# A one-core transformer step on Trainium2: modulation blocks at other units, inverse sums four at a time, w_o loaded from inside the attention loop

## What is computed

```python
shift1, scale1, gate1, shift2, scale2, gate2 = jnp.split(mod, 6, axis=-1)   # mod = silu(c) @ w_ada + b_ada
h = rmsnorm(x, norm1) * (1 + scale1) + shift1
q_a, kv_a, k_r, u = jnp.split(h @ w_in, ...)
q = rmsnorm(q_a, q_norm) @ w_qb                    # 8 heads, 64 plain + 32 rotary columns
k_nope, v = split(rmsnorm(kv_a, kv_norm) @ w_kvb)  # rotary on q_rope, k_rope for latent tokens
attn = softmax(q @ k.T * ATTN_SCALE) @ v           # latent: over latent and cached context keys
pooled = pool_mix(u, w_pool, pool_scale)
x = x + gate1 * (concat(attn, pooled) @ w_o)
h2 = rmsnorm(x, norm2) * (1 + scale2) + shift2
x = x + gate2 * (square(relu(h2 @ w1)) @ w2)       # w1 is 1024 x 4096
```

## Time and profile before

| | us |
|---|---|
| Device time, median of 3 runs | 1407.33 |
| Lowest and highest | 1406.74, 1409.57 |
| The profiled execution | 1411.18 |
| Its span in the profile | 1409.4 |
| Opening | 0 to 187 |
| Attention loop | 187 to 484 |
| Output projection | 484 to 590 |
| MLP | 590 to 1409 |

### The profile page before, as it was taken

How to read it: one execution, slowest core, us unless ns; L and a number is a source line. 1 busy time by engine, 2 the same in 40 slices (tenths; PEclk the granted TensorE clock), 3 DMA queues, 4 the chain that set the end, 5 groups by cost and what they waited for, 6 DMA issues and landing times.

```text
span 1409.4 us, 20531 instructions
## 1 busy us (share of the span) xinstructions
PE 1366.4 (97%) x7548; PEld 1229.6 (87%) x7548; DVE 789.5 (56%) x1074; ACT 715.8 (51%) x1537; POOL 444.4 (32%) x533
## 2 busy tenths in 40 slices
PE   7999989999999899999999999999999999999996
PEld 1899879999998778899998889999999999999995
DVE  4777567777787634355554456544444565444444
ACT  4867578888888623233333443433334443333332
POOL 3366648888888444430000003100000030000002
PEclk9999899999999999999999999999999999999998
DMA  9431101111111430344443333533333334333321
GB/s 343 148 100 53 35 5 44 43 40 44 43 39 39 139 138 1 127 175 172 168 154 122 115 119 122 190 119 119 133 135 120 120 120 165 138 129 119 119 89 45
DMA packets 50493, 154.50 MB, mean 110 GB/s; under 512 B 9848, under 2 KB 12440, under 8 KB 50424
## 3 DMA queue, kind: packets, MB, share of 16 engines
q1 hardware_dynamic: 49560, 150.47, 30.6%
q0 software_dynamic: 864, 3.15, 0.5%
HBM read 148.60 MB, written 4.83 MB: 109 GB/s over the span
## 4 chain that ended last, share of the span: by engine, by line
PE 64%; POOL 1%; DMA 1%; DVE 0%; issue 0%; ACT 0%; DVEq 0%; POOLq 0%
PE bank L2075 29%; PE bank L2083 28%; PE bank L1796 6%; DMA x<-in_w_o 1%; PE bank L1558 1%; POOL x L1866 0%; PE bank L2097 0%; DVE wol L1753 0%; POOL stat L1870 0%; POOL stat L1890 0%; ACT woh L1722 0%; DVE x L2026 0%; DVE xn L2014 0%; POOL stat L1872 0%; DVEq L1807 0%
## 5 line engine op out<-in xcount | busy, mean ns | idle before, releaser
L2075 PE MATMUL bank<-h2h,w1l 128*128 128x384 f32 x768 | 258.3, 336 | 0.0
L2075 PE MATMUL bank<-h2l,w1h 128*128 128x384 f32 x768 | 258.2, 336 | 0.0
L2075 PE MATMUL bank<-h2h,w1h 128*128 128x384 f32 x768 | 258.1, 336 | 0.0
L1866 POOL TENSOR_TENSOR x<-x,xn 128x512 f32<-128x512 f32 x12 | 20.6, 1745 | 726.6 <-DVE rTl L1984 499.8
L1973 DVE TENSOR_TENSOR w2l<-w2raw,w2h 128x1024 fp32r<-128x1024 f32 x95 | 118.7, 1249 | 169.5 <-ACT w2h L1904 169.5
L1904 ACT ACTIVATE w2h<-w2raw 128x1024 fp32r<-128x1024 f32 x95 | 100.8, 1061 | 191.4 <-PE bank L2083 191.4
L1911 ACT ACTIVATE relu<-bank 128x384 f32<-128x384 f32 x94 | 46.1, 491 | 287.6 <-PE bank L2075 287.6
L2083 PE MATMUL bank<-w2h,rTh 128*128 128x512 f32 x576 | 181.8, 396 | 0.0
L2083 PE MATMUL bank<-w2l,rTh 128*128 128x512 f32 x576 | 179.3, 392 | 0.0
L2083 PE MATMUL bank<-w2h,rTl 128*128 128x512 f32 x576 | 178.2, 390 | 0.0
L1980 DVE TENSOR_TENSOR sq<-relu 128x384 f32<-128x384 f32 x96 | 57.2, 596 | 179.5 <-ACT relu L1911 174.6
(11 more groups left out here) (272 smaller groups left out, 2783.0 us busy)
## 6 DMA issues: line engine op xcount, KB each, us to landing
w1raw<-in_w SPq DMA_DIRECT2D x96, 512.0 KB, 3.7
w2raw<-in_w SPq DMA_DIRECT2D x96, 512.0 KB, 4.6
ada_raw<-in_w_ada SPq DMA_DIRECT2D x24, 512.0 KB, 5.7
xn<-in_w_ada SPq DMA_DIRECT2D x16, 512.0 KB, 3.5
xin<-in_x SPq DMA_DIRECT2D x9, 512.0 KB, 3.8
x<-in_x SPq DMA_DIRECT2D x3, 1536.0 KB, 9.3
g_raw<-in_w_ada SPq DMA_DIRECT2D x8, 512.0 KB, 4.2
x<-in_w_o SPq DMA_DIRECT2D x6, 512.0 KB, 5.7
```

Of the source, the lines that this page charges most:

```text
L1866: nc.gpsimd.tensor_tensor(k.x[:, t, cut], k.x[:, t, cut], gated_half(t, i), ALU.add).then_inc(out_added, 1)
L2075: op = nc.tensor.matmul(bank[6 + s][:, 0:BN], w[0][s][x][:, c * P:(c + 1) * P], k.h2[b % 2][y_][:, c, :], start=n == 0, stop=n == 3 * DC - 1)
```

## The change

`ADA_AT` goes from (4, 7, 11, 14, 19, 22, 27, 30, 35, 38, 43, 46, 51, 54, 58, 61) to (4, 7, 11, 14, 19, 22, 25, 28, 32, 35, 38, 41, 46, 49, 52, 55), and `MOD_AT` from units 18, 34, 50, 64 to 18, 31, 44, 59. The inverse sums of four units are taken together, in every fourth unit, by three POOL operations on four columns; `turn_query` waits for POOL's own finished work in place of a count of the sums (`own_done`). `w_o` goes into the room of `x`, which is laid over buffers that the loop no longer needs then: pieces 0 to 3 are issued at unit 57, 4 to 6 at unit 58, the last at the loop's end. The latent gate vector goes out to DRAM at unit 3 and is read back as a broadcast at the start of the closing function, in place of PE's spread and ACT's two copies. The last of the half reads, with its add and its product, moves from the loop's end into the closing function. In the first output tile PE takes, for each piece, high by high, high by low of the activations (behind `wo_hi`, which ACT gives), then the low part of `w_o` (behind `wo_ready`). POOL's mixer parts and the turned attention are made two tiles ahead in place of one.

```diff
         k.mixT = sbr("mixT", [P, G, NTOK])
+        with ExitStack() as ahead:
+            k.x = memory(nc, ahead)("x", [P, T, D])
+        k.gate_rows = nc.dram_tensor("gate_rows", [1, D], F32, kind="Internal").ap()
...
-            k.x = sb("x", [P, T, D])
+            sb("x_place", [P, T, D])
...
+        k.out_l, k.inv_all = out_l, inv_all
...
         LAST = NU + 4
+        W_O_AT = {57: range(0, 4), 58: range(4, DC - 1)}
...
-        ADA_AT = {u: r for r, u in enumerate((4, 7, 11, 14, 19, 22, 27, 30, 35, 38, 43, 46, 51, 54, 58, 61))}
-        MOD_AT = {18: 0, 34: 1, 50: 2, 64: 3}
+        ADA_AT = {u: r for r, u in enumerate((4, 7, 11, 14, 19, 22, 25, 28, 32, 35, 38, 41, 46, 49, 52, 55))}
+        MOD_AT = {18: 0, 31: 1, 44: 2, 59: 3}
...
                     at = 4 * n % 8
-                    sp.wait_ge(rs_ready, 8 * n + 8)
+                    sp.wait_ge(rs_ready, 3 * n + 3)
...
-                    sp.dma_start(inv_all[:, :], inv_rows[n:n + 1, :].to_broadcast([VD, 512])).then_inc(rs_moved, 16)
+                    if n < NPAIR // 2 - 1:
+                        sp.dma_start(inv_all[:, :], inv_rows[n:n + 1, :].to_broadcast([VD, 512])).then_inc(rs_moved, 16)
+                        return
+                    sp.wait_ge(k.wo_loaded[2], 32)
+                    sp.dma_start(inv_all[:, :], inv_rows[n:n + 1, :].to_broadcast([VD, 512])).then_inc(k.wo_loaded[2], 16)
...
                         spread(u // 4 - 1)
+                    if u == 3:
+                        sp.wait_ge(gain_done, 6)
+                        sp.dma_start(k.gate_rows[0].rearrange("(c p) -> p c", p=P), k.mod[:, 2 * DC:3 * DC, 0],
+                                     allow_slow_non_contiguous=True).then_inc(stored, 16)
+                    if u in W_O_AT:
+                        sp.wait_ge(side_filled, len(sides))
+                        for n in W_O_AT[u]:
+                            if n >= 4:
+                                sp.wait_ge(k.wo_loaded[n % 4], 16)
+                            sp.dma_start(k.x[:, n, :], a["w_o"][W_O[n]]).then_inc(k.wo_loaded[n % 4], 16)
+                sp.wait_ge(stored, 48)
                 sp.wait_ge(mod_read, 2 * (NADA // 4))
-                for n in range(2):
-                    sp.dma_start(k.xn[:, n, :], a["w_o"][W_O[n]]).then_inc(k.wo_loaded[n], 16)
+                sp.wait_ge(k.wo_loaded[3], 16)
+                sp.dma_start(k.xn[:, 0, :], a["w_o"][W_O[DC - 1]]).then_inc(k.wo_loaded[3], 16)
...
+                def own_done(u):
+                    begun = [4 * r + 2 for v, r in ADA_AT.items() if v < u] + [4 * r + 4 for v, r in ADA_AT.items() if v + 2 < u]
+                    if begun:
+                        pool.wait_ge(ada_sums, max(begun))
+                    heads = 2 + sum(v % LT == 2 for v in range(u) if v // LT + 2 < H)
+                    pool.wait_ge(wh_ready, heads)
+                    if u >= 4:
+                        pool.wait_ge(rs_ready, 3 * (u // 4))
+                    rows_ctx = [(v - 1) // LT for v in range(1, u + 1) if ctx_now(v - 1, "scores")]
+                    if rows_ctx:
+                        pool.wait_ge(c_ready, 2 * max(rows_ctx) + 2)
                 def turn_query(n, u):
                     f = qf[n % 2]
-                    pool.wait_ge(rs_ready, 2 * u)
+                    pool.wait_ge(q_lo, n)
+                    own_done(u)
...
-                def inverse_sum(u):
-                    x = u % 8
-                    pool.wait_ge(p_exp, 3 * u + 3)
-                    if u >= 8:
-                        pool.wait_ge(rs_moved, 32 * (u // 4 - 2) + 16)
-                    nc.gpsimd.tensor_scalar(rs[:, x:x + 1], psum[:, x, 0:1], psum[:, x, 1:2], psum[:, x, 2:3], ALU.add, ALU.add).then_inc(rs_ready, 1)
-                    pool.wait_ge(rs_ready, 2 * u + 1)
-                    nc.gpsimd.tensor_tensor(rs[:, x:x + 1], rs[:, x:x + 1], k.minus[:, :], ALU.pow).then_inc(rs_ready, 1)
+                def inverse_sums(g):
+                    x = slice(4 * g % 8, 4 * g % 8 + 4)
+                    pool.wait_ge(p_exp, 12 * g + 12)
+                    if g >= 2:
+                        pool.wait_ge(rs_moved, 32 * (g - 2) + 16)
+                    nc.gpsimd.tensor_tensor(rs[:, x], psum[:, x, 0], psum[:, x, 1], ALU.add).then_inc(rs_ready, 1)
+                    pool.wait_ge(rs_ready, 3 * g + 1)
+                    nc.gpsimd.tensor_tensor(rs[:, x], rs[:, x], psum[:, x, 2], ALU.add).then_inc(rs_ready, 1)
+                    pool.wait_ge(rs_ready, 3 * g + 2)
+                    nc.gpsimd.tensor_tensor(rs[:, x], rs[:, x], k.minus[:, :].to_broadcast([P, 4]), ALU.pow).then_inc(rs_ready, 1)
...
                     h, s = divmod(u, LT)
-                    if u:
-                        inverse_sum(u - 1)
+                    if u and u % 4 == 0:
+                        inverse_sums(u // 4 - 1)
...
                     if u >= 8:
-                        act.wait_ge(rs_ready, 2 * u - 14)
+                        act.wait_ge(rs_ready, 3 * (u // 4) - 3)
...
                     n = half_read(u)
-                    if n is not None:
+                    if n is not None and n < NPAIR // 2 - 1:
...
                     n = half_read(u)
+                    if n == NPAIR // 2 - 1:
+                        n = None
...
                         modulation(MOD_AT[u])
-                spread_gate(nc, pe, k, 2, 0, bank[0:2])
...
-def spread_gate(nc, pe, k, section, j, out):
-    for c in range(DC):
-        op = nc.tensor.matmul(out[c // 4][:, (c % 4) * P:(c % 4 + 1) * P],
-                              k.mod[:, section * DC + c, j:j + 1].to_broadcast([P, P]), k.ident[:, :], start=True, stop=True)
-    return op
-def read_gate(nc, act, gate, out, done):
-    for i in range(2):
-        op = nc.scalar.activation(gate[:, i * 512:(i + 1) * 512], out[i][:, :], ACT.Copy)
-    op.then_inc(done, 1)
...
-        wor = [k.xn[:, 0, :], k.xn[:, 1, :]] + [k.x[:, t, :] for t in range(3, T)]
+        wor = [k.x[:, n, :] for n in range(DC - 1)] + [k.xn[:, 0, :]]
...
-        spread_ready, spread_done, gain2_done = sem("gate_ready"), sem("gate_done"), sem("gain2_done")
+        gate1_loaded, spread_ready, attn_last = sem("gate1_loaded"), sem("gate_ready"), sem("attn_last")
...
         def out_sync(sp):
-            for n in range(2, DC):
-                if n >= 4:
-                    sp.wait_ge(wo_loaded[n % 4], 16 * (n // 4))
-                sp.dma_start(wor[n], a["w_o"][W_O[n]]).then_inc(wo_loaded[n % 4], 16)
+            sp.dma_start(gate1[:, 0, :], k.gate_rows[0:1, :].to_broadcast([P, D])).then_inc(gate1_loaded, 16)
             for i in range(3):
-                if i:
-                    sp.wait_ge(wo_ready, 2 + 3 * i)
+                sp.wait_ge(wo_ready, min(3 * i + 3, DC - 1))
...
             pool.wait_ge(wo_ready, DC - 2)
+            mixer(1)
             for t in range(T):
-                if t + 1 < T:
-                    mixer(t + 1)
+                if t + 2 < T:
+                    mixer(t + 2)
...
             turned(1)
-            read_gate(nc, act, gate1[:, 0, :], bank[0:2], spread_done)
             act.wait_ge(spread_ready, 1)
-            read_gate(nc, act, gate1[:, 1, :], bank[6:8], spread_done)
+            for i in range(2):
+                nc.scalar.activation(gate1[:, 1, i * 512:(i + 1) * 512], bank[i][:, :], ACT.Copy)
+            nc.scalar.activation(k.out_l[:, :], bank[6][VD:P, :], ACT.Copy).then_inc(attn_last, 1)
             for t in range(T):
-                if 1 < t + 1 < T:
-                    turned(t + 1)
+                if t + 2 < T:
+                    if t + 2 == LT // 2:
+                        act.wait_ge(attn_last, 3)
+                    turned(t + 2)
...
                 nc.vector.scalar_tensor_tensor(k.gain2[:, :, j], k.mod[:, 4 * DC:5 * DC, j], 1.0, k.cols[:, C_N2:C_N2 + DC],
-                                               ALU.add, ALU.mult).then_inc(gain2_done, 1)
-            dve.wait_ge(spread_done, 2)
+                                               ALU.add, ALU.mult)
+            dve.wait_ge(gate1_loaded, 16)
+            dve.wait_ge(attn_last, 1)
             for t in range(T):
-                if 1 < t + 1 < T:
-                    turned(t + 1)
...
                                             ALU.mult).then_inc(gated, 1)
+                if t == 0:
+                    dve.wait_ge(wo_loaded[2], 48)
+                    nc.vector.tensor_tensor(k.out_l[:, :], bank[6][0:VD, :], k.out_l[:, :], ALU.add).then_inc(attn_last, 1)
+                    dve.wait_ge(attn_last, 2)
+                    nc.vector.tensor_tensor(k.attn[VD:2 * VD, H // 2 - 1, 512:LAT].rearrange("p (i q) -> p i q", i=4),
+                                            k.inv_all.rearrange("p (q i) -> p i q", i=4),
+                                            k.out_l[:, :].rearrange("p (i q) -> p i q", i=4), ALU.mult).then_inc(attn_last, 1)
+                if t + 2 < T:
+                    turned(t + 2)
...
         def out_tensor(pe):
```

(17 more changed lines are left out.)

## The result

| | us |
|---|---|
| The changed kernel, median of 4 runs | 1424.95 (1422.89 to 1426.37) |
| The kernel before on the same chip, median of 4 runs | 1408.45 (1406.74 to 1409.63) |
| Ratio, with its 95% interval | 1.0118 (1.0101 to 1.0134) |
| Forecast, with its range | 1412.5 (1400 to 1418) |
| The profiled execution of the changed kernel, and its span | 1426.14, 1424.4 |

The change made the kernel slower by 16.5 us. Slower had been forecast, but by 5.2, and the time lies outside the forecast range. The places that were named are the right ones; what a stall costs there was put too low.

The account below looks back on a forecast made before the run. PE was taken to set the attention loop's pace, ACT and POOL close behind. 13.8 lost − 3.7 (last head) − 0.3 (unit 33's stall) − 4.6 (boundary, first tile) = +5.2 us, 1412.5 on the median; range 1400 to 1418.

Parts of the forecast that it names:

- The places that were named: Attention loop: late modulation blocks at units 25, 28, 38, 41, 49, 52, 55, and unit 8's turn, make PE wait.
- what a stall costs there: Attention loop: PE stalls of 2.0 us at block 25, 2.2 at 28, 3.3 at 41, 3.7 at 55; 13.8 in all.

Follow-up runs that it names:

- two otherwise unchanged kernels: The kernel before with ACT's half read repeated three and six times more at units 27 and 43, or four and five: 1416.51 and 1413.71 us.
- The fastest kernel here: Changed kernel with old block and matmul places, `w_o` at units 62 and 63, latent multiply behind half read, context adds one unit later: 1401.84 us.

## What to carry to other kernels

When moved side work makes PE wait, add the lower clock behind the wait to the price; at the two long stalls here it added 2.9 and 3.1 us to waits of 4.2 and 2.3. Look at what stands in series with the moved work (a load that waits for the last user of its buffer) and compare that chain, not the busy time, with the new spacing. And before moving work out of a stretch to make room for a transfer, try the transfer later: with `w_o` five units on and the blocks left where they were the rest of the change gained 4.4 us, where with the blocks moved it lost 16.5. And price a moved piece at the slot it comes to: the same 16 matmuls made a unit 1.0 us longer at one slot and 1.4 to 1.9 at others.

## What the hardware showed that was not expected

In two otherwise unchanged kernels, in one profiled execution each, 3.2 us of idle PE brought 2.4 us more, by a granted clock of 0.52 over the next six; 1.6 us brought nothing, 2.0 us brought 1.3 and 2.7 us nothing. The fastest kernel here shows the same between its executions: 1400.6 to 1401.7 at a mean clock of 0.993 to 0.995 (six of twelve) and 1405.7 to 1407.9 at 0.988 to 0.990 (four). Raising to a power on POOL took 0.56 us for 128x1 and 1.04 for 128x4, while an add of two operands on 128x4 took 0.20, less than the 0.37 that the form with two adds took on 128x1. A 512 KB load behind four others in one queue took 8.4 us from issue to use in place of 3.9. A POOL cast of 0.61 us that met a row of DVE instructions took 3.29 or 3.30 in all eight profiles with the changed closing part.
